# Branch A's attention in slots of one tile, each with a half block of projection

## The chip, the cores and the metric

One core of a Trainium2 chip runs the whole kernel. The time is that of the device for one launch, in microseconds (us), as the median of several runs. The engines named below: TensorE (PE, matmuls; PEld is its weight load), VectorE (DVE), ScalarE (ACT), GpSimd (POOL) and SyncE (SP, whose queue issues the DMAs).

## The reference

A layer with three attention branches over 1024 tokens (two groups of 512) of width 1024. What matters here is branch A, differential attention with 4 heads (the kernel's units), each with two softmax maps over 64 columns, and the gating of each branch:

```python
h = rms_norm(x, pre_g)
u = h @ w_in        # aq ak av ag | bq bk bv bg | cq ck cv cg | mg
logits = einsum('bqhmd,bkhmd->bhmqk', qb, k) * scale + bias      # branch A
p = softmax(logits, axis=-1)
attn = p[:, :, 0] - lam * p[:, :, 1]
o = einsum('bhqk,bkhe->bqhe', attn, v)
ya = rms_norm(o, subln_g) * (1.0 - lambda_init) * silu(ag)
m = gates[0] * (ya @ wa) + gates[1] * (yb @ wb) + gates[2] * (yc @ wc)
x = x + rms_norm(m @ w_out, post_g)
```

Then branches B (grouped queries with rotary embedding) and C (neighbourhood attention), an output projection and an embedding follow.

## The kernel before

Every float32 operand of a matmul is split into a high part and a low part, and a product is three passes: high by high, high by low, low by high. A weight block (128 x 1024) comes by DMA into one of two `stage` slots (`load_w`, L304), ScalarE casts it into `w_hi` (`split_w`, L996 to L1002), GpSimd subtracts to get `w_lo` (`split_w`, L445 to L450). The blocks are numbered: 16 of branch A (query, key, value, gate of 4 units), then key, query 0 and value of branch B, then the blocks of the three merges (a gate projection and a branch projection for each of 8 chunks). A program is written for each engine, and its instructions run in the order written; semaphores with counts join the engines.

`project` (L586) makes one block: 8 chunks k, each with 3 parts by 2 groups of 512 tokens, 48 passes, into two banks of PSUM. A unit of branch A in `attend_qkv` (L667) and `finish` (L699) has eight query tiles of 128. For each tile:

- `score` (L602): six matmuls into two banks, which of two pairs by the tile's parity
- VectorE `find_max` (L1368): bias added and maximum taken (L1383) twice, then the small negation of the two maxima (L1388)
- ScalarE `exp_probs` (L1007, L1017), VectorE `scales` (reciprocal, L1394, and the product with lambda, L1397), ScalarE `scale_second` (L1038), VectorE `norm_probs` (L1411)
- TensorE `turn_probs` (L615, L618): four transposes
- ScalarE `probs_hi` (L1029) and VectorE `probs_lo` (the subtraction of L1355)

With the tiles come the passes of the unit's own gate block in the shares of `GATE_SHARES_A` (one or two of 8 chunks in a tile). The blocks of query, key and value of the next unit stand behind the tiles, in `finish` and behind it, with `mix_group` (L663), which mixes the values of a group by the turned tiles, between them, and `sum_squares` (L713) last. The three units in a loop and the last one are written at L791 to L801. In the last unit the blocks are those of branch B.

Behind the units (L802 to L838): GpSimd takes the power of all 32 columns of the squares' sums (`inv_sqrt`, L433, L482), then of the 16 of the keys' heads, then splits the next gate blocks. VectorE makes eight diagonals (L1634), TensorE spreads them by a product with ones (L819) between the chunks of a block, and VectorE normalises y (L1641). Two gate blocks of merge A and three turns follow, the keys' rotated turn (L827) ahead of the second gate block (L831). ScalarE and VectorE split keys, values and y (`split_y`) while that block runs. Then `merge_branch` and `merge_rest` (L743) alternate branch products and gate blocks; the first gate block of `merge_rest` is the third of the merge.

## Time and profile before

| | |
|---|---|
| median of 3 runs | 1528.74 us (1524.14 to 1530.47) |
| span of the profiled execution | 1522.4 us |
| PE busy | 1411.3 us, 93% |
| DVE busy | 602.4 us, 40% |
| ACT busy | 536.9 us, 35% |
| POOL busy | 291.8 us, 19% |
| TensorE in the chain that ended last | 84% of the span |

The busy time is of one profiled execution; matmuls are pipelined, so that a matmul of about 0.39 us is followed by the next after 0.23 us, and distances between starts tell what a pass costs. "Idle before, releaser" in a row is the time for which the engine stood before the instruction, and whom it waited for. The granted clock is a share of 2.4 GHz: at 0.5 TensorE runs at 1.2 GHz.

### The profile page before, as it was taken

How to read it: one execution, taken by the hardware profiler on the slowest of the kernel's cores; microseconds unless marked ns; L12 is line 12 of the kernel's file. 1: busy time of each engine (PE TensorE's matmuls, PEld its weight loads, DVE VectorE, ACT ScalarE, POOL GpSimd, SP SyncE). 2: the span in 40 equal slices, each digit the busy share in tenths (PEclk: the TensorE clock that was granted, in tenths of full speed). 3: DMA queues.
4: the chain of work that ended last, by engine and by line, in shares of the span. 5: the costliest groups of instructions: out<-in, count | busy, mean ns of one | idle time of the engine just before them, and what ended most of it. 6: DMA issues, size and time to landing. Idle time of an engine off the chain costs nothing.

```text
span 1522.4 us, 18598 instructions
## 1 busy us (share of the span) xinstructions
PE 1411.3 (93%) x6780; PEld 1129.2 (74%) x6780; DVE 602.4 (40%) x1062; ACT 536.9 (35%) x977; POOL 291.8 (19%) x173
## 2 busy tenths in 40 slices
PE   5999999999999798987999898989898999899998
PEld 3767677677887576765788786878787888788887
DVE  5272635546300646456212125152525212544332
ACT  4262534432111536446211115252524212324432
POOL 1211202131222113020022131111211112213100
PEclk9999999999999999998999999999999999999999
DMA  5111101011111000000011110111000113322200
GB/s 185 57 36 36 49 21 49 28 45 46 42 42 55 28 14 28 14 14 8 21 43 61 55 56 23 46 34 34 34 28 29 42 42 138 111 82 70 69 35 35
DMA packets 25746, 71.77 MB, mean 47 GB/s; under 512 B 2872, under 2 KB 4792, under 8 KB 25568
## 3 DMA queue, kind: packets, MB, share of 16 engines
q1 hardware_dynamic: 25696, 71.09, 13.9%
q8 instruction: 33, 0.54, 0.2%
q14 instruction: 17, 0.14, 0.0%
HBM read 66.86 MB, written 4.23 MB: 47 GB/s over the span
## 4 chain that ended last, share of the span: by engine, by line
PE 84%; DVE 8%; ACT 3%; issue 3%; POOL 1%; DMA 0%; SPq 0%; DVEq 0%; ACTq 0%; POOLq 0%
PE ps L581 45%; PE ps L738 9%; PE ps L633 7%; PE ps L952 6%; PE ps L934 6%; PE ps L618 3%; PE ps L611 3%; ACT s L1017 2%; DVE s L1383 2%; PE ps L598 2%; PE ps L958 1%; DVE pt_lo L1355 1%; DVE stat L1388 1%; PE ps L764 1%; POOL small L436 1%
## 5 line engine op out<-in xcount | busy, mean ns | idle before, releaser
L450 POOL TENSOR_TENSOR w_lo<-stage,w_hi 128x1024 fp32r<-128x1024 f32 (+1 forms) x92 | 194.4, 2113 | 923.8 <-ACT w_hi L1002 922.6
L581 PE MATMUL ps<-h_hi,w_hi 128*128 128x512 f32 x1040 | 335.8, 404 | 4.2 <-ACT s L1017 1.9
L581 PE MATMUL ps<-h_lo,w_hi 128*128 128x512 f32 x1040 | 324.3, 393 | 0.0
L581 PE MATMUL ps<-h_hi,w_lo 128*128 128x512 f32 x1040 | 323.7, 393 | 0.0
L581 PEld LDWEIGHTS ps<-h_hi,w_hi 128*128 128x128 f32 x1040 | 188.6, 189 | 59.2 <-issue 19.7
L581 PEld LDWEIGHTS ps<-h_lo,w_hi 128*128 128x128 f32 x1040 | 196.5, 189 | 44.5
L581 PEld LDWEIGHTS ps<-h_hi,w_lo 128*128 128x128 f32 x1040 | 196.3, 189 | 43.3
L1002 ACT CAST w_hi<-stage 128x1024 fp32r<-128x1024 f32 (+1 forms) x92 | 86.0, 935 | 298.2 <-PE ps L581 213.1
L1029 ACT CAST pt_hi<-ps 128x512 fp32r<-128x512 f32 (+2 forms) x160 | 77.6, 525 | 167.6 <-PE ps L618 103.6
L1355 DVE TENSOR_TENSOR pt_lo<-ps,pt_hi 128x512 fp32r<-128x512 f32 (+2 forms) x160 | 91.3, 603 | 113.9 <-ACT pt_hi L1029 113.9
L618 PE MATMUL ps<-ident,s 128*128 128x128 f32 x544 | 85.6, 288 | 51.5 <-DVE pt_lo L1355 34.4
L618 PEld LDWEIGHTS ps<-ident,s 128*128 128x128 f32 x544 | 63.9, 146 | 80.7 <-DVE pt_lo L1355 32.1
L1383 DVE CUSTOM_DVE_ANT_0 s<-ps,tables 128x512 f32<-128x512 f32 (+2 forms) x128 | 70.5, 588 | 91.3 <-PE ps L611 64.0
L1017 ACT ACTIVATE s<-s,stat 128x512 f32<-128x512 f32 (+2 forms) x128 | 81.2, 636 | 55.0 <-DVE stat L1388 54.6
L1502 DVE SCALAR_TENSOR_TENSOR s<-s,ps 128x1024 f32<-128x1024 f32 x16 | 19.5, 1221 | 190.1 <-PE ps L738 190.1
L633 PE MATMUL ps<-pt_hi,v_hi 128*128 128x512 f32 (+2 forms) x192 | 71.0, 370 | 9.1 <-DVE pt_lo L1355 4.8
L738 PE MATMUL ps<-pt_hi,w_hi 128*128 128x512 f32 x192 | 61.7, 404 | 10.3 <-DVE m L1504 8.9
L633 PE MATMUL ps<-pt_lo,v_hi 128*128 128x512 f32 (+2 forms) x192 | 69.1, 360 | 0.0
L633 PE MATMUL ps<-pt_hi,v_lo 128*128 128x512 f32 (+2 forms) x192 | 68.6, 357 | 0.0
L1038 ACT ACTIVATE s<-s,stat 128x512 f32<-128x512 f32 (+2 forms) x96 | 65.0, 677 | 4.4 <-DVE stat L1394 4.4
L738 PE MATMUL ps<-pt_hi,w_lo 128*128 128x512 f32 x192 | 60.9, 399 | 0.0
L738 PE MATMUL ps<-pt_lo,w_hi 128*128 128x512 f32 x192 | 60.7, 398 | 0.0
(173 smaller groups left out, 1881.6 us busy)
## 6 DMA issues: line engine op xcount, KB each, us to landing
stage<-in_w_gates SPq DMA_DIRECT2D x24, 512.0 KB, 3.2
stage<-in_w_qkvg_a SPq DMA_DIRECT2D x19, 512.0 KB, 3.2
stage<-in_w_qkvg_c SPq DMA_DIRECT2D x16, 512.0 KB, 3.2
stage<-in_w_branch SPq DMA_DIRECT2D x24, 256.0 KB, 2.7
m<-in_x_tok SPq DMA_DIRECT2D x4, 1024.0 KB, 9.4
y<-in_x_tok SPq DMA_DIRECT2D x8, 512.0 KB, 3.4
stage<-in_w_pg SPq DMA_DIRECT2D x16, 256.0 KB, 2.7
out<-y SPq DMA_DIRECT2D x16, 256.0 KB, 2.0
```

Of the source, the lines that this page charges most:

```text
L450: nc.gpsimd.tensor_tensor(dst, stage[:, slot, 0:width], f32(hi), ALU.subtract).then_inc(w_ready, 1)
L581: done = mm(ps[:, bank + g, :], w[:, slot, k * P:(k + 1) * P], h[:, k, g * SEQ:(g + 1) * SEQ], start=first and part == 0, stop=last and pa ...
L618: done = nc.tensor.transpose(ps[:, e if both else t % 2, k * P:(k + 1) * P], s[:, t % 2, e, k * P:(k + 1) * P], ident[:, :])
L633: done = mm(ps[:, 2 + g, q0 * P:q1 * P], v[:, g * QT + k, e * HD:e * HD + P], p[:, e if both else g, k, q0 * P:q1 * P], start=n == 0, stop ...
L738: done = mm(ps[:, 2 + g, :], w[:, slot, c * P:(c + 1) * P], yy[:, c * TOK + g * SEQ:c * TOK + (g + 1) * SEQ], start=c == 0 and part == 0, ...
L934: done = mm(ps[:, 2 * c + nb, :], a[:, k * P:(k + 1) * P], w[:, k, nb * 512:(nb + 1) * 512], start=k == 0 and part == 0, stop=k == KC - 1 ...
L952: mm(ps[:, c, :], a[:, k * P:(k + 1) * P], w[:, k * 512:(k + 1) * 512], start=k == 0 and part == 0, stop=k == KC - 1 and part == 2)
L1002: nc.scalar.copy(dst, stage[:, slot, 0:width]).then_inc(w_hi_done, 1)
L1017: done = nc.scalar.activation(dst, src, ACT.Exp, bias=stat[:, t % 2, 2 + e:3 + e], accum_out=stat[:, t % 2, 4 + e:5 + e])
L1029: nc.scalar.copy(*turned_probs(pt_hi, j, near, both, e)) \
L1355: sub = lambda out, whole, hi: nc.vector.tensor_tensor(out, whole, f32(hi), ALU.subtract)
L1383: done = nc.vector.tensor_tensor_reduce(out=s[:, t % 2, e, 0:width], in0=ps[:, 4 + 2 * (t % 2) + e, 0:width], in1=bias[:, e, first:first + ...
```

## The change

Branch A is cut into 32 tile slots without a loop. A slot has the next tile's score, 24 passes (one group's half of a block of the next half unit: query, key, value, gate in slots 0 to 3 of a half), and the turn of the slot's own tile. A block's weights are thus used by one group at a time and are loaded, cast and split twice, once for each group (32 blocks of A where there were 16). Scores use one pair of banks, projections banks 6 and 7 in turn, and the mix of a half stands at the end of its fourth slot. Sums, powers, diagonals and the normalisation of y are made per half or per unit, inside the slots of the next unit; the last two of the eight are left for the tail. The bias is kept in two places by turns, the second in `m`. The last four slots carry branch B's key block and the first gate block of merge A. In the tail stand the value block, the query block, and the second gate block, now ahead of the three turns. `LATER` in place of `LEAD` is a count's offset only.

TensorE:

```diff
+            def project_a(slot, chunks):
+                half, j = block_of(slot)
+                n, g, bank = N_A + 4 * half + j, half % 2, 6 + j % 2
+                if 0 in chunks:
+                    pe.wait_ge(w_ready, LEAD + n + 1)
...
+                    if j == 0:
+                        pe.wait_ge(v_ready, LEAD + half)
+                    if j == 1:
+                        pe.wait_ge(gate_ready, LEAD + half)
...
+                for k in chunks:
+                    for part, (w, h) in enumerate([(w_hi, h_hi), (w_hi, h_lo), (w_lo, h_hi)]):
+                        done = mm(ps[:, bank, :], w[:, n % 2, k * P:(k + 1) * P], h[:, k, g * SEQ:(g + 1) * SEQ],
+                                  start=k == 0 and part == 0, stop=k == KC - 1 and part == 2)
...
+            def turn_values_a(half):
+                g = half % 2
+                pe.wait_ge(plain, LEAD + half + 1)
...
+            def score_a(tile):
...
+                if tile >= 1:
+                    pe.wait_ge(maxed, LEAD + tile)
...
+            def turn_tile_a(tile):
+                pe.wait_ge(normed, LEAD + tile + 1)
+                if tile >= 2:
+                    pe.wait_ge(pt_ready, LEAD + tile - 1)
...
+            def mix_a(half):
...
+                pe.wait_ge(v_ready, LEAD + half + 1)
+                pe.wait_ge(pt_ready, LEAD + 4 * half + 4)
+                mix(g, False, False)
...
+            def spread_rstd(c, bank):
+                pe.wait_ge(diag_ready, LEAD + c + 1)
+                if c == 0:
+                    pe.wait_ge(ones_ready, LEAD + 1)
+                pe.wait_ge(y_normed, LEAD + c)
...
+            def attend_a(tile):
+                half, j = divmod(tile, 4)
+                u, t = divmod(tile, 8)
+                fill = project_a if tile < A_TILES - 4 else project_next
+                if tile + 1 < A_TILES:
+                    score_a(tile + 1)
+                if j < 3:
+                    fill(tile, range(0, KC // 2))
+                    if j == 1 and half >= 1:
+                        sum_squares(half - 1)
+                    if u >= 1 and t in (4, 5):
+                        spread_rstd(2 * (u - 1) + t - 4, 3)
+                    fill(tile, range(KC // 2, KC))
+                    turn_tile_a(tile)
+                else:
+                    fill(tile, range(0, 2))
+                    if half + 1 < A_HALVES:
+                        turn_values_a(half + 1)
+                    fill(tile, range(2, 5))
+                    turn_tile_a(tile)
+                    fill(tile, range(5, KC))
+                    mix_a(half)
...
+            project_a(-3, range(KC))
+            project_a(-2, range(KC))
+            score_a(0)
+            project_a(-1, range(0, 4))
+            turn_values_a(0)
+            project_a(-1, range(4, KC))
+            for tile in range(A_TILES):
+                attend_a(tile)
+            pe.wait_ge(w_ready, LEAD + N_KQV + 3)
+            pe.wait_ge(maxed, LEAD + A_TILES)
+            for k in range(KC):
+                done = project_part(0, 4, k, k == 0, k == KC - 1)
+                if k == 3:
+                    pe.wait_ge(pt_ready, LEAD + A_TILES)
+                    turn(rope_buf, 0, turned)
+                if k == 5:
+                    sum_squares(A_HALVES - 1)
...
+            pe.wait_ge(w_ready, LEAD + N_KQV + 4)
+            pe.wait_ge(mg_tanh, LEAD + 1)
             for k in range(KC):
                 done = project_part(1, 6, k, k == 0, k == KC - 1)
+                if k == 4:
+                    pe.wait_ge(ss_saved, LEAD + A_HALVES)
+                    spread_rstd(A_HALVES - 2, 2)
+                if k == 6:
+                    spread_rstd(A_HALVES - 1, 3)
...
-            project(N_MERGE[0], 1, 4)
+            pe.wait_ge(plain, LATER + UNITS + 2)
+            project(N_MERGE[0] + 1, 0, 4)
             pe.wait_ge(roped, LEAD + 1)
             turn(rope_buf, 0, rope_turned)
-            pe.wait_ge(y_normed, LEAD + 8)
+            pe.wait_ge(y_normed, LEAD + A_HALVES)
             turn(vg, 2, turned)
-            pe.wait_ge(plain, LEAD + UNITS + 3)
-            project(N_MERGE[0] + 1, 0, 6)
-            pe.wait_ge(k_ready, LEAD + UNITS + 1)
+            pe.wait_ge(plain, LATER + UNITS + 3)
+            pe.wait_ge(k_ready, LATER + UNITS + 1)
             turn(rope_buf, 0, turned)
```

GpSimd:

```diff
+            for n in range(4 * A_HALVES):
+                split_w(N_A + n, n % 2)
+                u, slot = divmod(n, 8)
...
+                if u + 1 < UNITS and slot in (6, 7):
+                    spread_bias_a(u + 1, slot - 6)
+                if u >= 1 and slot == 7:
+                    square_root_a(u - 1)
+            split_w(N_KQV, 0)
+            split_w(N_KQV + 1, 1)
+            split_w(N_KQV + 2, 0)
             pool.wait_ge(mixed, LEAD + 2 * UNITS)
...
+            square_root_a(UNITS - 1)
...
             pool.wait_ge(head_var, LEAD + 1)
             inv_sqrt(head_rstd, head_ss, head_pow)
-            for f in range(2):
-                split_w(N_MERGE[0] + f, 1 - f)
+            split_w(N_KQV + 3, 1)
+            split_w(N_MERGE[0] + 1, 0)
```

ScalarE:

```diff
+            def attend_a(tile):
+                half, j = divmod(tile, 4)
+                if j != 0:
+                    probs_hi_a(tile - 1)
+                if tile <= A_TILES - 4:
+                    take_block_a(*block_of(tile - 1))
+                else:
+                    take_next(tile - 1)
+                if tile < A_TILES - 4:
+                    split_w(N_A + tile + 5, (tile + 1) % 2, (tile + 5) // 2 + 1)
+                if tile == A_TILES - 4:
+                    split_w(N_KQV + 1, 1, N_KQV // 2 + 1)
+                if tile == A_TILES - 2:
+                    split_w(N_KQV + 2, 0, N_KQV // 2 + 2)
+                if j == 0 and half >= 1:
+                    square_output(half - 1)
+                if tile + 1 < A_TILES:
+                    exp_a(tile + 1)
+                    scale_second_a(tile + 1)
+                if j == 3:
+                    if half + 1 < A_HALVES:
+                        values_hi_a(half + 1)
+                    probs_hi_a(tile)
```

VectorE:

```diff
+            def attend_a(tile):
+                half, j = divmod(tile, 4)
+                u, t = divmod(tile, 8)
+                if tile + 1 < A_TILES:
+                    find_max_a(tile + 1)
+                if j != 0:
+                    probs_lo_a(tile - 1)
+                if tile <= A_TILES - 4:
+                    take_block_a(*block_of(tile - 1))
+                if tile + 1 < A_TILES:
+                    scales_a(tile + 1)
+                    norm_probs_a(tile + 1)
+                if j == 0 and half >= 1:
+                    take_y_a(half - 1)
+                if j == 2 and half >= 1:
+                    save_squares(half - 1)
+                if u >= 1 and t in (3, 4):
+                    diagonal(2 * (u - 1) + t - 3)
+                if u >= 1 and t in (5, 6):
+                    normalize_y(2 * (u - 1) + t - 5, 3)
+                if j == 3:
+                    if half + 1 < A_HALVES:
+                        values_lo_a(half + 1)
+                    probs_lo_a(tile)
```

SyncE loads the weights of A in the order of the 32 half blocks, each waiting for the split of the block two before, with the bias rows between them:

```diff
+            for n in range(2, 4 * A_HALVES):
+                load_w(N_A + n, n % 2, w_qkvg_a[4 * (n // 8) + n % 4])
+                u, slot = divmod(n, 8)
+                if n == 3:
+                    load_raw_a(0, 1)
+                if u + 1 < UNITS and slot in (5, 7):
+                    load_raw_a(u + 1, slot // 6)
```

## Rows read from the trace of the kernel before

**Rows 1.** Windows (start:end us, length, busy PE PEld DVE ACT POOL, clock, DMA); a PE gap.

```profile
69.00:334.46 265.46, 249.85 (x1216) 192.14 (x1213) 133.26 (x313) 122.50 (x234) 43.82 (x23) 0.97 0.11 38
...
870.00:874.00 4.00, 3.52 (x9) 2.80 (x10) 0.43 (x1) 0.00 (x0) 0.00 (x0) 0.57 0.38 131
...
870.48 1.22 PE L738 MATMUL ps<-pt_hi,w_hi 128*128 128x512 f32 x2 [4.69 <-DVE m L1504]
```

**Rows 2.** Waits of TensorE, 40 to 560 us (us in total, times, longest).

```profile
PE ps L618 <- DVE s L1411: 9.0, 8, 1.8
```

**Rows 3.** Chain of work that ended last (start us, us, what).

```profile
168.37 5.51 PE ps L581 x24
...
180.27 2.74 PE ps L633 x12
...
207.70 1.68 PE ps L720 x16
...
340.40 0.89 DVE m L1634 x4
...
393.19 10.99 PE ps L581 x48
```

**Rows 4.** Timeline of PE in unit 1 (start us, us, instruction): turn, score, projection.

```profile
152.57 0.60 PE L618 MATMUL ps<-ident,s 128*128 128x128 f32 x4
153.10 0.50 PE L611 MATMUL ps<-k_hi,q_hi 64*128 64x512 f32 x2
...
153.99 0.74 PE L581 MATMUL ps<-h_hi,w_hi 128*128 128x512 f32 x2
```

**Rows 5.** Timelines of ScalarE and GpSimd: the second weight block's cast and subtraction.

```profile
39.38 1.05 ACT L1002 CAST w_hi<-stage 128x1024 fp32r<-128x1024 f32 x1
...
40.51 2.38 POOL L450 TENSOR_TENSOR w_lo<-stage,w_hi 128x1024 fp32r<-128x1024 f32 x1 [11.52 <-ACT w_hi L1002]
```

**Rows 6.** Timelines of PE and DVE: unit 1's first score, maximum, negation.

```profile
139.90 0.50 PE L611 MATMUL ps<-k_hi,q_hi 64*128 64x512 f32 x2
...
141.16 0.69 DVE L1383 CUSTOM_DVE_ANT_0 s<-ps,tables 128x512 f32<-128x512 f32 x1 [0.88 <-PE ps L611]
...
142.50 0.17 DVE L1388 TENSOR_SCALAR stat<-stat 128x2 f32<-128x2 f32 x1
```

**Rows 7.** Timelines of PE and ACT: a turn and its copy.

```profile
148.24 0.65 PE L618 MATMUL ps<-ident,s 128*128 128x128 f32 x4 [1.74 <-DVE v_lo L1355]
...
148.93 0.59 ACT L1029 CAST pt_hi<-ps 128x512 fp32r<-128x512 f32 x1 [1.05 <-PE ps L618]
```

**Rows 8.** Timelines of POOL and DVE; last, line 1411's durations (ns min/median/max).

```profile
157.44 2.38 POOL L450 TENSOR_TENSOR w_lo<-stage,w_hi 128x1024 fp32r<-128x1024 f32 x1 [28.36 <-ACT w_hi L1002]
...
158.28 1.57 DVE L1388 TENSOR_SCALAR stat<-stat 128x2 f32<-128x2 f32 x1
...
161.43 0.17 DVE L1394 RECIPROCAL stat<-stat 128x2 f32<-128x2 f32 x1 [0.34 <-ACT s L1017]
...
L1411 DVE SCALAR_TENSOR_TENSOR s<-s,stat x32: 737/746/2382, 74.9 to 314.7; 128x512 f32<-128x512 f32 x32
```

**Rows 9.** Timelines of four engines behind the units, up to the merge.

```profile
334.95 8.28 POOL L436 TENSOR_TENSOR small<-small 128x32 f32<-128x32 f32 x2 [8.00 <-DVE small L1366]
...
372.48 1.04 PE L598 MATMUL ps<-ident,tables 128*128 128x128 f32 x8
...
376.79 1.05 ACT L1138 ACTIVATE s<-ps 128x1024 f32<-128x1024 f32 x1
...
378.81 4.63 DVE L1355 TENSOR_TENSOR pt_lo<-y,pt_hi 128x1024 fp32r<-128x1024 f32 x4 [1.15 <-ACT pt_hi L1132]
...
387.77 1.03 ACT L1066 ACTIVATE y<-ps 128x1024 f32<-128x1024 f32 x1 [6.16 <-PE ps L598]
...
389.81 2.41 POOL L450 TENSOR_TENSOR w_lo<-stage,w_hi 128x1024 fp32r<-128x1024 f32 x1 [11.52 <-ACT w_hi L1002]
```

**Rows 10.** The page's DMA issues (KB each, us to landing).

```profile
stage<-in_w_qkvg_a SPq DMA_DIRECT2D x19, 512.0 KB, 3.2
```

More of the change, by code:

```diff
@@ new lines, in sum_squares @@
+            def sum_squares(half):
+                g = half % 2
+                pe.wait_ge(y_ready, LEAD + half + 1)
+                for qt in range(QT):
+                    done = mm(ps[:, 2 + g, 2 * qt:2 * qt + 2], y_squares[g][:, qt * P:(qt + 1) * P], ones2,
+                              start=True, stop=True)
+                done.then_inc(ss_done, 1)
+            def spread_rstd(c, bank):
[3 more added lines that the diff above has]
+                pe.wait_ge(y_normed, LEAD + c)
+                for qt in range(QT):
+                    done = mm(ps[:, bank, qt * P:(qt + 1) * P], ones_sq, diagonals[c % 2][:, qt * P:(qt + 1) * P],
+                              start=True, stop=True)
+                done.then_inc(spread, 1)
@@ L812, in _ @@
-            pe.wait_ge(ones_ready, LEAD + 1)
-            squares_taken(UNITS)
-            pe.wait_ge(w_ready, LEAD + N_KQV + 3)
-            for c in range(2 * UNITS):
-                pe.wait_ge(diag_ready, LEAD + c + 1)
-                pe.wait_ge(y_normed, LEAD + c - 1)
-                for qt in range(QT):
-                    done = mm(ps[:, 2 + c % 2, qt * P:(qt + 1) * P], ones_sq,
-                              diagonals[c % 4][:, qt * P:(qt + 1) * P], start=True, stop=True)
-                done.then_inc(spread, 1)
-                done = project_part(0, 4, c, c == 0, c == KC - 1)
@@ new lines, in exp_a, with scale_second_a @@
+            def exp_a(tile):
+                act.wait_ge(maxed, LEAD + tile + 1)
+                for e in range(2):
+                    dst = s[:, tile % 2, e, :]
+                    done = nc.scalar.activation(dst, dst, ACT.Exp, bias=stat[:, tile % 2, 2 + e:3 + e],
+                                                accum_out=stat[:, tile % 2, 4 + e:5 + e])
+                done.then_inc(exped, 1)
+            def scale_second_a(tile):
+                act.wait_ge(scales_ready, LEAD + tile + 1)
+                p1 = s[:, tile % 2, 1, :]
+                nc.scalar.mul(p1, p1, stat[:, tile % 2, 8:9]).then_inc(scaled, 1)
@@ new lines, in scales_a, with norm_probs_a @@
+            def scales_a(tile):
+                st = stat[:, tile % 2, :]
+                dve.wait_ge(exped, LEAD + tile + 1)
+                steps.done(dve, nc.vector.reciprocal(st[:, 6:8], st[:, 4:6]))
+                nc.vector.tensor_tensor(st[:, 8:9], st[:, 7:8], lam, ALU.mult).then_inc(scales_ready, 1)
+            def norm_probs_a(tile):
+                st = stat[:, tile % 2, :]
+                p0, p1 = s[:, tile % 2, 0, :], s[:, tile % 2, 1, :]
+                dve.wait_ge(scaled, LEAD + tile + 1)
+                stt(out=p0, in0=p0, scalar=st[:, 6:7], in1=p1, op0=ALU.mult, op1=ALU.subtract).then_inc(normed, 1)
@@ new lines, in save_squares, with diagonal @@
+            def save_squares(half):
+                dve.wait_ge(ss_done, LEAD + half + 1)
+                nc.vector.tensor_copy(a_ss[:, 4 * half:4 * half + 4], ps[:, 2 + half % 2, 0:8:2]).then_inc(ss_saved, 1)
+                if half % 2 == 1:
+                    dve.wait_ge(ss_saved, LEAD + half + 1)
+                    mean_square(a_ss[:, 4 * half - 4:4 * half + 4], P, a_var)
+            def diagonal(c):
+                dve.wait_ge(y_pow, LEAD + c // 2 + 1)
+                if c == 0:
+                    dve.wait_ge(x_turned, LEAD + TILES)
+                if c >= 2:
+                    dve.wait_ge(spread, LEAD + c - 1)
+                for qt in range(QT):
+                    done = nc.vector.tensor_scalar(diagonals[c % 2][:, qt * P:(qt + 1) * P], ident[:, :],
+                                                   a_rstd[:, 4 * c + qt:4 * c + qt + 1], None, ALU.mult)
+                done.then_inc(diag_ready, 1)
```

487 lines of the change are left out of this document (287 added, 200 removed).

## The prediction, made before the changed kernel was run

> **What bounds the kernel now.** I read the windows by stage first. From 69.00 to 334.46, the four units of branch A, TensorE is busy 249.85 of 265.46 us at a granted clock of 0.97 [rows 1]. So at most 15.6 us of idle time is to be had there, and some 3.4 us of clock (about four of the 4 us windows at 0.57 to 0.80, where matmuls run at 1.2 instead of 2.4 GHz). The waits of TensorE say who ends the idle time: the turn of a tile waits for the normalised tile, 9.0 us in 8 waits [rows 2]. VectorE and ScalarE run a serial chain per tile that the eight tile slots of a unit hardly cover, while the long stretches after them leave both idle. The change spreads the projections evenly over the slots. Everything up to 393.19, where the third gate projection of merge A begins in the kernel before [rows 3], is touched; behind it the code is the same. I work out when that projection starts in the changed kernel.
>
> **TensorE's work is conserved.** A turn takes 0.53 us to the next score (153.10 - 152.57), a score 0.89 us to the projection behind it (153.99 - 153.10), 24 passes 5.51 us, and restarting them costs about 0.1 us (estimate, from the first pair's length) [rows 3, 4]. A slot is then 0.53 + 0.89 + 5.51 + 0.1 = 7.03 us. The passes work on one group instead of two, so each pair of passes no longer shares a weight; but the mix, where each pass has its own weights, runs at 2.74 / 12 = 0.228 us a pass, the projection at 5.51 / 24 = 0.230 [rows 3]. Nothing is added there. The loop: 32 slots 225.0; less the last score 1.0; seven half turns of values at 0.5, 3.5; eight mixes at 2.8, 22.4; seven sums of squares at 1.68 / 2 and a restart, 6.3; six spreads at 1.0 (half the passes of a sum, 0.84, and restarts), 6.0 [rows 3]. Sum 262.2 us.
>
> **The ramp.** The first half block is done at about 39.8 as before. K's block needs the weights whose low part GpSimd finishes at 40.51 + 2.38 = 42.9 [rows 5]; before, TensorE had the second group of the first block to do meanwhile. K and V, 5.6 each, end at 54.1; score 0, 0.9; half of the gate block, 2.8, to 57.8. The turn of the values waits for a copy that stands behind tile 0's exponentials on ScalarE: their maximum comes at about 56.7, collides with a weight split (below) until 57.7, 1.5 for the exponentials, 0.5 for the copy, so 59.8, a 2.0 us wait. Then 0.5 + 2.8: slot 0 starts at 63.0. Loop without waits: to 63.0 + 262.2 = 325.2.
>
> **The chain in a slot, and what it meets.** Count from the start of a slot's score (S). The maximum starts at S + 1.26 (141.16 - 139.90), the small negation behind it at S + 2.60 (142.50) [rows 6]. Meanwhile ScalarE: the turn before is 0.53 old at S and its copy starts 0.69 after it (148.93 - 148.24), S + 0.16; some 0.5 later (the copy lasts 0.59) that of the projected block, as much later the weight cast, and GpSimd's subtraction starts 1.13 after a cast (40.51 - 39.38), S + 2.25 [rows 5, 7]. It runs 2.4 us. The trace shows what a negation does then: it started at 158.28 inside the subtraction of 157.44 to 159.82 and took 1.57 instead of 0.17 us, to 159.85; over the trace the normalisation's length, too, goes from 737 to 2382 ns [rows 8]. Before, that happens once a unit; now each slot but the last few has a weight subtraction at that place, 0.35 us ahead of the negation. The negation ends at S + 4.7, the reciprocal follows 1.58 later (161.43 - 159.85) [rows 8], the scaling of the second map ends at S + 7.5, the normalisation at S + 8.2. Without the collision it is S + 6.2. Either fits, since the tile is wanted a slot later.
> The Trainium skill, page SBUF — State Buffer, section Who interferes with whom, says that an operation of VectorE in a 2-port mode such as tensor_scalar, and GpSimd, take a shared port pair as an exclusive lock, whoever issues first. The trace agrees, the negation above. By that page it is the order of issue that decides; were there no such lock, the first rival's time would hold.
>
> **Two places where TensorE waits for the end of that chain.**
> First, the fourth slot of each half: VectorE splits the values and the fourth turned tile behind the next tile's normalisation, and the mix stands on it. 8.2 + 0.7 + 0.7 = S + 9.6 against TensorE's arrival: score 0.9, 24 passes 5.6, turns 0.5 and 0.5, S + 7.5. That is 2.2 us with the wake-up, seven times (the last half has no next tile): 15.4. In three of them a diagonal (0.89 us [rows 3]) stands ahead too, but GpSimd's power shifts its subtraction there; between 0 and 2.6, I take 1.3.
> Second, slot 5 of units 1 to 3: both spreads of the past unit use bank 3, so the second waits for the first to be normalised, which VectorE does behind slot 5's own normalisation. TensorE comes there at S + 0.9 + 2.9 + 0.9 = 4.7; the normalisation of y ends at S + 8.2 + 0.7 = 8.9 with the collision, 6.9 without. Two slots at 4.3 and one, in the last unit where no weights are cast, at 2.2: 10.8. After a gap of 4.69 us the clock was 0.57 for 4 us [rows 1]: the level of 1.2 GHz for most of them. Such a gap costs about 1.5 us more, twice: 3.0. A copy of K's block adds 0.4. The loop ends at 325.2 + 15.4 + 1.3 + 10.8 + 3.0 + 0.4 = 356.1.
>
> **What follows the loop.** V's block with a turn (0.9), the last sum (0.9) and restarts: 13.0. The query's weights stand in GpSimd's queue behind two powers. The sum starts at 9.2 after the loop, is saved and scaled by 10.8; powers of 32 and 16 columns take 8.28 together [rows 9], so 8 and 16 take 1.5 and 2.8, with the squares' reduction (1.2) between them hidden by half; subtraction 2.4 (2.41 in [rows 9]). Ready at 17.7: a wait of 4.7, and 1.5 of clock. Query block with two spreads 13.0, gate block 11.0: the turn of the rotated keys starts 43.2 after the loop. Before, a gate block of 11 us stood behind that turn and covered ScalarE and VectorE; now it stands ahead. Before, the first y_lo came 378.81 - 372.48 = 6.33 after the turn, 0.92 of it a tanh that is gone, and four took 4.63 [rows 9]: the last at 10.05. Then ScalarE squares and casts, and the third gate's weights are ready 389.81 + 2.41 - 387.77 = 4.45 later [rows 9]: 14.6, with wake-ups 15.0. The gate starts at 356.1 + 43.2 + 15.0 = 414.3, 21.1 later than 393.19.
> Branch A's weights once more are 16 loads of 512 KB and 3.2 us to landing each [rows 10], one per slot of 7 us and asked for two slots ahead: hidden. SyncE's bias rows stand between them; raw rows take about 5 us and have two slots. The 16 more casts (0.94) and subtractions (2.4) lie beside TensorE, and cost what the collision costs. The bias of two units in two places lets the spreading run early: nothing on the path.
>
> **Sum.** 1522.4 + 21.1 = 1543.5 span; the median of the runs is 6.3 above the profiled span (1528.74 - 1522.4): 1549.8, **1550 us**.
>
> **Rivals.** *No collision* (0.19): the negation slips in ahead of the subtraction, which decides from 0.35 us of shift in my reading [rows 6, 7]. Mix waits 0.2 x 7, slot 5's 2.2 x 3, clock none: the loop ends at 63.0 + 262.2 + 1.4 + 6.6 + 0.4 = 333.6, the gate starts at 391.8, and the time is 1527: not slower. For it: the difference of two paths each read to 0.1 us. Against: ScalarE starts each slot early.
> *The pipeline is full* (0.12): I have a wait wrong, TensorE never waits in the loop: 325.2 + 58.2 = 383.4, -9.8, 1519; if the tail's waits (4.7 + 1.5) go too, 1513. For it: the sum of engine time per slot is far under 7 us on ScalarE and VectorE. Against: the order of each queue, above.
> *More of it* (0.14): clock lost at each mix gap too (7 x 1.5 = 10.5), the diagonals in full (1.3), GpSimd's copies of the bias in the way (3 x 1): 1565.
> The change does what it says in all of them; that it doesn't is no case, the slots are written out.
>
> **How the numbers follow.** My case 0.55, around 1550 (1542 to 1557 by itself). A measurement tells about 0.5% from no change, 7.6 us: 1521.1 to 1536.4. Slower: 0.55 + 0.14 = 0.69. Same: no collision, less the 0.02 in which it ends below, 0.17, and a sixth of the full pipeline, 0.02: 0.19. Faster 0.12. For 8 in 10 the range goes from the no-collision case less 6 us, 1521, to 1563.
>
> **What would show it.** In the profile after: waits of TensorE at the mix for VectorE's pt_lo, seven near 2.2 us; in slot 5 of units 1 to 3 a wait of the spread for VectorE's y, 4.3 us; a wait of about 5 us for a weight subtraction behind V's block; the negation lengthened to near 2.2 us in most slots. First score near 54, slot 0 at 63, the loop's end near 356. If the negation is 0.17 us in most slots, my case is wrong and the first rival right; if TensorE's idle time between 63 and the merge is under 10 us, the second is.

## The result and the profile after

The changed kernel takes **1551.29 us** (median of 4 runs, 1551.13 to 1551.55) against 1529.01 for the kernel before on the same chip (4 runs, 1524.14 to 1530.47): a ratio of 1.0161, 95% interval 1.0140 to 1.0182. It is slower by 1.6%; 1550 was predicted. The profiled execution has a span of 1549.2 us where before had 1522.4, so 26.8 us more. The times of the kernel before fall in two groups (in the comparisons of the experiments 26 runs at 1522.7 to 1526.3 with a granted clock of 0.970 to 0.975, and 16 at 1528.4 to 1532.0 with 0.966 to 0.969), so its median moves by a few us from one comparison to the next, and the profiled execution belongs to the first group.

The page of the changed kernel: busy time of each engine; the chain that ended last, by engine; the traffic to and from HBM; the weight loads of branch A (KB each, us to landing).

```profile
PE 1420.4 (92%) x6780; PEld 1135.2 (73%) x6780; DVE 629.0 (41%) x1085; ACT 556.0 (36%) x1015; POOL 328.0 (21%) x192
...
PE 80%; DVE 10%; ACT 5%; issue 3%; POOL 1%; DMA 0%; SPq 0%; DVEq 0%; ACTq 0%; POOLq 0%
...
HBM read 75.25 MB, written 4.23 MB: 51 GB/s over the span
...
stage<-in_w_qkvg_a SPq DMA_DIRECT2D x35, 512.0 KB, 3.3
```

The share of TensorE in the chain fell from 84 to 80%. The doubled loads are 35 instead of 19 [rows 10] and land as fast as before, 3.3 us; none of the waits of TensorE from 40 to 440 us has a DMA for its releaser. The waits of TensorE from 40 to 440 us (us in total, times, longest) answer to [rows 2]:

```profile
PE ps L667 <- DVE pt_lo L1579: 12.7, 7, 2.1
PE ps L846 <- DVE y L1795: 10.7, 3, 4.2
PE ps L615 <- POOL w_lo L468: 5.2, 2, 4.5
PE ps L763 <- POOL w_lo L468: 3.1, 1, 3.1
...
PE ps L791 <- ACT vg L1237: 1.9, 1, 1.9
...
PE ps L781 <- ACT tables L1251: 0.4, 1, 0.4
```

The 9.0 us for turns in [rows 2] are gone. In their place the mix (L667) stands seven times for the low parts, the spread (L846) three times for y, and there are waits for GpSimd's weights at the ramp (L763) and behind the loop (L615). The 1.9 us (L791) are the first turn of the values, and the 0.4 us (L781) are for ScalarE's copy of branch B's key block. A slot with the 4.2 us wait, and the negation over the whole trace, from the timelines of GpSimd, VectorE and TensorE (start us, us, instruction, idle time before and releaser); the last line gives ns min/median/max:

```profile
177.36 2.40 POOL L468 TENSOR_TENSOR w_lo<-stage,w_hi 128x1024 fp32r<-128x1024 f32 x1 [10.65 <-ACT w_hi L1132]
...
177.69 2.10 DVE L1718 TENSOR_SCALAR stat<-stat 128x2 f32<-128x2 f32 x1
...
184.08 2.05 PE L846 MATMUL ps<-m 128*128 128x128 f32 x8 [4.20 <-DVE y L1795]
...
L1718 DVE TENSOR_SCALAR stat<-stat x32: 168/2094/2312, 58.1 to 344.9; 128x2 f32<-128x2 f32 x32
```

The negation of two columns starts 0.33 us inside GpSimd's subtraction and ends with it, 2.10 us long. That was one tile in eight before; now the median of all 32 is 2.09 us. Chain of the work that ended last, changed kernel (start us, us, what), from the ramp to branch B; it answers to [rows 3]:

```profile
42.83 12.87 PE ps L763 x48
55.70 0.92 PE ps L808 x6
...
64.85 0.90 PE ps L808 x5
...
358.55 5.50 PE ps L615 x24
...
375.80 9.92 PE ps L615 x30
...
417.36 11.24 PE ps L615 x48
...
523.67 0.89 PE ps L632 x8
...
527.95 5.94 PE ps L615 x18
```

Line 55.70 is score 0, 64.85 slot 0's score, 358.55 the end of the loop of slots, and 417.36 the third gate block of merge A, which stood at 393.19 [rows 3]: 24.2 us later. Merge A itself ends 24.4 later (523.67 against 499.23), the first unit of branch B adds some 2.3, and from there the distance stays (merge C's start 892.85 against 865.90: 26.95).

### The profile page after: what moved, and what is told of

It reads as the page before. It is cut to its first block, busy times and chain, and to the rows that moved or that the text cites. A ratio compares the mean times of both kernels' runs of the same rounds, so it can differ in the third digit from the quotient of the medians.

```text
span 1549.2 us, 18441 instructions
## 1 busy us (share of the span) xinstructions
PE 1420.4 (92%) x6780; PEld 1135.2 (73%) x6780; DVE 629.0 (41%) x1085; ACT 556.0 (36%) x1015; POOL 328.0 (21%) x192
## 4 chain that ended last, share of the span: by engine, by line
PE 80%; DVE 10%; ACT 5%; issue 3%; POOL 1%; DMA 0%; SPq 0%; DVEq 0%; ACTq 0%; POOLq 0%
PE ps L615 34%; PE ps L888 8%; PE ps L667 8%; PE ps L763 7%; PE ps L1081 6%; PE ps L1063 6%; PE ps L652 3%; PE ps L645 2%; DVE pt_lo L1579 2%; DVE stat L1718 2%; ACT s L1269 2%; PE ps L808 2%; PE ps L632 2%; PE ps L1087 1%; PE ps L781 1%
## 5 line engine op out<-in xcount | busy, mean ns | idle before, releaser
L468 POOL TENSOR_TENSOR w_lo<-stage,w_hi 128x1024 fp32r<-128x1024 f32 (+1 forms) x108 | 232.3, 2152 | 911.0 <-ACT w_hi L1132 910.8
L615 PE MATMUL ps<-h_hi,w_hi 128*128 128x512 f32 x768 | 246.3, 402 | 7.2 <-POOL w_lo L468 5.2
L615 PE MATMUL ps<-h_lo,w_hi 128*128 128x512 f32 x768 | 239.9, 394 | 0.0
L615 PE MATMUL ps<-h_hi,w_lo 128*128 128x512 f32 x768 | 239.6, 393 | 0.0
L1132 ACT CAST w_hi<-stage 128x1024 fp32r<-128x1024 f32 (+1 forms) x108 | 103.0, 955 | 307.3 <-PE ps L615 211.2
L615 PEld LDWEIGHTS ps<-h_hi,w_hi 128*128 128x128 f32 x768 | 140.7, 189 | 43.8 <-issue 9.9
L615 PEld LDWEIGHTS ps<-h_lo,w_hi 128*128 128x128 f32 x768 | 145.2, 189 | 32.7
L615 PEld LDWEIGHTS ps<-h_hi,w_lo 128*128 128x128 f32 x768 | 145.4, 189 | 32.2
L763 PE MATMUL ps<-h_hi,w_hi 128*128 128x512 f32 x256 | 107.5, 420 | 6.4 <-POOL w_lo L468 6.4
L1159 ACT CAST pt_hi<-ps 128x512 fp32r<-128x512 f32 (+2 forms) x128 | 59.1, 511 | 134.7 <-PE ps L652 69.7
L763 PE MATMUL ps<-h_hi,w_lo 128*128 128x512 f32 x256 | 102.5, 400 | 0.0
L763 PE MATMUL ps<-h_lo,w_hi 128*128 128x512 f32 x256 | 101.8, 398 | 0.0
L667 PE MATMUL ps<-pt_hi,v_hi 128*128 128x512 f32 (+2 forms) x192 | 71.7, 373 | 21.8 <-DVE pt_lo L1579 17.6
L888 PE MATMUL ps<-pt_hi,w_hi 128*128 128x512 f32 x192 | 62.4, 408 | 12.7 <-DVE m L1844 8.9
L1269 ACT ACTIVATE s<-s,stat 128x512 f32<-128x512 f32 x64 | 45.7, 716 | 71.7 <-DVE stat L1718 71.7
L667 PE MATMUL ps<-pt_lo,v_hi 128*128 128x512 f32 (+2 forms) x192 | 69.7, 363 | 0.0
L667 PE MATMUL ps<-pt_hi,v_lo 128*128 128x512 f32 (+2 forms) x192 | 69.2, 360 | 0.0
L763 PEld LDWEIGHTS ps<-h_hi,w_hi 128*128 128x128 f32 x256 | 49.3, 193 | 26.4 <-issue 10.7
```

What stands on the lines that cost most here:

```text
L468: nc.gpsimd.tensor_tensor(dst, stage[:, slot, 0:width], f32(hi), ALU.subtract).then_inc(w_ready, 1)
L615: done = mm(ps[:, bank + g, :], w[:, slot, k * P:(k + 1) * P], h[:, k, g * SEQ:(g + 1) * SEQ], start=first and part == 0, stop=last and pa ...
L667: done = mm(ps[:, 2 + g, q0 * P:q1 * P], v[:, g * QT + k, e * HD:e * HD + P], p[:, e if both else g, k, q0 * P:q1 * P], start=n == 0, stop ...
L763: done = mm(ps[:, bank, :], w[:, n % 2, k * P:(k + 1) * P], h[:, k, g * SEQ:(g + 1) * SEQ], start=k == 0 and part == 0, stop=k == KC - 1 a ...
L888: done = mm(ps[:, 2 + g, :], w[:, slot, c * P:(c + 1) * P], yy[:, c * TOK + g * SEQ:c * TOK + (g + 1) * SEQ], start=c == 0 and part == 0, ...
L1132: nc.scalar.copy(dst, stage[:, slot, 0:width]).then_inc(w_hi_done, 1)
```

## The experiments

The times are medians; each ratio is to the kernel before on the same chip in the same comparison (1525.78 us of 20 runs for the first four, 1524.77 of 13 for the next four, 1524.97 of 9 for the last two). The ratio of the changed kernel is 1.0161. "Loop excess" is the distance from slot 0's score to the loop's end, less the 262.2 us that the prediction summed for TensorE's own work in it.

**1. The negation in a form that the subtraction does not block** (changed kernel).

```diff
-nc.vector.tensor_scalar(st[:, 2:4], st[:, 0:2], -1.0, None, ALU.mult).then_inc(maxed, 1)
+nc.vector.tensor_reduce(st[:, 2:4], st[:, 0:2].unsqueeze(2), AX.X, ALU.max,
+                        negate=True).then_inc(maxed, 1)
```

> The changed kernel, with the negation behind each maximum of branch A (line 1718, a tensor_scalar that lasts 2.1 to 2.3 us in most slots) written as a tensor_reduce with negate; nothing else. My theory (the collision with GpSimd's weight subtraction sets the end of the chain): the negation lasts under 0.3 us in every slot, TensorE's wait at the mix falls from 12.7 us in 7 to under 3, its wait for y in slot 5 from 4.2 to about 2.2 us in the first two units, and the time falls by 12.7 - 2 + 4 + 3 (clock) = 17 to 19 us, to 1533. Rival (the collision fills slack that the chain has anyway, and the chain is simply too long for a slot): no more than 3 us are gained, 1548 or more. Rival (the doubled loads, casts and subtractions cost by themselves): no change, 1551.

Measured: 1531.54 us (1530.75 to 1533.18), ratio 1.0034 (1.0019 to 1.0049); span 1529.9, 19.3 less than the changed kernel's. Negation (ns), then TensorE's waits from 40 to 440 us:

```profile
L1718 DVE TENSOR_REDUCE stat<-stat x32: 154/155/156, 58.7 to 326.3; 128x2 f32<-128x2 f32 x32
...
PE ps L846 <- DVE y L1796: 6.8, 3, 2.3
...
PE ps L667 <- DVE pt_lo L1579: 2.2, 3, 0.7
```

The subtractions are all still there, 2.4 us each, and at the same place: in the slot shown above the reduction starts at 183.32 in a subtraction of 183.00 to 185.42, and takes 0.15. The mix waits drop from 12.7 to 2.2 and those for y from 10.7 to 6.8, 2.3 at the longest (predicted for this case: 0.2 and 2.2 each). Without the collision 19.8 of the some 25 us of loss are gone.

**2. y normalised at the head of its slot** (changed kernel): on VectorE the normalisation of y stands ahead of the next tile's maximum, no longer behind the tile's normalisation. The collision stays.

```diff
+if u >= 1 and t in (5, 6):
+    normalize_y(2 * (u - 1) + t - 5, 3)
 if tile + 1 < A_TILES:
     find_max_a(tile + 1)
 ...
-if u >= 1 and t in (5, 6):
-    normalize_y(2 * (u - 1) + t - 5, 3)
```

> The changed kernel, with VectorE's normalisation of y in slots 5 and 6 of units 1 to 3 moved from behind that slot's chain to the head of the slot; nothing else. My theory (two spreads share bank 3, and the second waits for a step queued behind slot 5's chain): the three waits of the spread for y (10.7 us in all, 4.2 at the longest) vanish, and the half-rate clock behind two or three of them with it (1.5 us each): 13.5 to 15 us less, 1537. Rival (the wait is only given on to the mix of the next slots, where the same chain is late): the mix's waits grow by what is gained and the time stays at 1549 or more.

Measured: 1534.43 us (1532.78 to 1538.63), ratio 1.0061 (1.0038 to 1.0085); span 1533.0. The wait of L846 is gone; the mix keeps its own:

```profile
PE ps L667 <- DVE pt_lo L1579: 12.8, 7, 2.1
```

The loop goes from 63.51 to 344.25, an excess of 18.5 us where the changed kernel has 31.5: 10.7 for the waits, and 2.3 net for the clock. Net, because the clock now falls behind three of the mix waits (0.76 from 128 to 132 us, 0.72 from 200, 0.68 from 272), where in the changed kernel it fell behind one. Of the 16.2 us of span another 1.3 came ahead of the loop and 1.9 behind it, where no edit lies: K's block took 11.27 instead of 12.87 us, and the 30 matmuls behind the wait for the query's weights 8.74 instead of 9.92. So the time, 2.6 us under the 1537 of the theory, holds about 3 us that the edit doesn't explain.

**3. Both.**

> Both edits together (negation as tensor_reduce, y normalised at the head of slots 5 and 6). My theory: TensorE's waits in the loop fall to under 5 us, the loop ends near 331, and the time is 1551 - 18 - 10 = 1522 to 1526 (the wait in slot 5 is counted once: what is left of it after the first edit is 3 x 2.2 and some clock). Rival (either edit uncovers a third wait of the same size): no better than the better of the two alone, 1532 or more.

Measured: 1519.68 us (1518.74 to 1521.73), ratio 0.9958 (0.9945 to 0.9972); span 1516.5. TensorE's wait at the mix (the only other one inside the loop is the 0.4 for the copy of the key block), and, from the chain, slot 0's score and the loop's end:

```profile
PE ps L667 <- DVE pt_lo L1579: 2.2, 3, 0.7
...
62.95 0.89 PE ps L808 x6
...
328.09 5.50 PE ps L615 x24
```

The loop takes 265.1 us, an excess of 2.9, of which 2.6 are these two waits. So 262.2 was right for TensorE's own work to 0.3 us, and the pipeline of slots does what it is for once the two places are cleared. It beats the kernel before, by 0.4%. The two edits bring 31.6 us together, where they bring 19.8 and 16.9 one by one: the long waits for y were made of both, the collision and the place in the queue. The 1522 to 1526 that were expected were too slow.

**4. A shorter subtraction.** Changed kernel; from the third block of branch A on, GpSimd subtracts 512 of 1024 columns, so that half of the low parts of those weights isn't made. The negation keeps its form.

```diff
-split_w(N_A + n, n % 2)
+split_w(N_A + n, n % 2, width=TOK if n < 2 else 512)
```

> The changed kernel, with GpSimd's subtraction for branch A's weights over 512 of 1024 columns from the third block on: the other half of the low parts isn't computed (old values are used). Loads, casts, matmuls and every wait stay. A dose of the suspected cause: a subtraction of 1.3 instead of 2.4 us still starts 0.3 us ahead of the negation. My theory: the negation lasts 1.0 to 1.2 instead of 2.1 to 2.3 us, the mix's seven waits fall by 1.1 each (7.5 us), slot 5's by 1.1 twice (2), with some of the clock: 10 us less, 1541. Rival (GpSimd's work doesn't matter): no change, 1551.

Measured: 1542.42 us (1540.25 to 1544.71), ratio 1.0115 (1.0087 to 1.0143); span 1538.0.

```profile
L1718 DVE TENSOR_SCALAR stat<-stat x32: 168/993/2101, 57.6 to 334.6; 128x2 f32<-128x2 f32 x32
...
PE ps L667 <- DVE pt_lo L1579: 8.9, 7, 2.7
PE ps L846 <- DVE y L1795: 8.5, 3, 3.1
```

The subtraction lasts 1.29 to 1.30 us and the median negation 0.99; the waits for y fall from 4.2 to 3.1 at the longest, by what the negation is shorter. The length of the wait follows the length of the subtraction, with the instruction on VectorE unchanged. The longest mix wait rose to 2.7, though. It is the last one (it ends at 309.98), and its negation is blocked for 2.09 us as before: it starts at 302.27, in a subtraction of 301.94 to 304.33 that belongs to branch B's key block and isn't shortened. In the changed kernel the same negation fell into the power ahead of that subtraction and took 0.17 us.

**5. The query's weights ahead of the powers on GpSimd** (changed kernel).

```diff
+split_w(N_KQV + 3, 1)
 square_root_a(UNITS - 1)
 ...
-split_w(N_KQV + 3, 1)
 split_w(N_MERGE[0] + 1, 0)
```

> The changed kernel, but on GpSimd the subtraction of the last query-weight block of branch A is issued ahead of the two powers of the last unit instead of behind them. In the changed kernel's trace the powers take 368.95 to 373.44, the subtraction 373.44 to 375.75, and TensorE waits 4.5 us for it; the clock is 0.50 in 376 to 380. Theory (the wait is queueing on GpSimd and nothing else): the wait of 4.5 goes, and with it the clock lost behind it (about 1.5), so the marker of merge A comes 5.5 to 6 us earlier and the time is 1545 to 1546; the powers, now 2.3 later, must not become a wait of the last turn. Rival 1 (ScalarE's cast of that block is just as late): the wait shrinks to 1 to 2 and the time is 1548 to 1549. Rival 2 (the branch's end is set by GpSimd's later subtractions, for the gate blocks, whatever stands before): the time stays at 1551.

Measured: 1540.47 us (1539.99 to 1543.04), ratio 1.0096 (1.0063 to 1.0130); span 1538.6, 10.6 less, where 6 was expected.

```profile
367.86 9.74 PE ps L615 x42
...
409.25 11.24 PE ps L615 x48
...
519.85 4.33 PE ps L615 x18
```

Between the sum of squares and the first spread lie 9.7 us here and 17.2 in the changed kernel (368.48 to 385.72): 7.5, of which 4.5 is the wait and 3.0 the clock. In the changed kernel the 30 matmuls behind the wait took 9.92 us, at 0.23 each they are 6.9: I had priced the clock at 1.5. The price isn't the same in every execution: behind the same wait of 4.5 us the 30 matmuls took 9.96 us in experiment 6, 9.47 to 9.59 in 1, 4 and 10, and 8.74 in 2 and 3. The marker comes 8.1 earlier. Of the rest, 1.6 us is in branch B's first unit: the same 18 matmuls take 4.33 instead of 5.94 us.

**6. The second gate block in halves around the turns** (changed kernel).

```diff
-project(N_MERGE[0] + 1, 0, 4)
+project(N_MERGE[0] + 1, 0, 4, range(0, KC // 2))
 pe.wait_ge(roped, LEAD + 1)
 turn(rope_buf, 0, rope_turned)
 pe.wait_ge(y_normed, LEAD + A_HALVES)
 turn(vg, 2, turned)
+project(N_MERGE[0] + 1, 0, 4, range(KC // 2, KC))
```

> The changed kernel, but the second gate block of merge A is issued in two halves: four chunks of rows ahead of the turns of the keys, four behind them, so that the chain of ScalarE and VectorE behind those turns lies beside TensorE's work. The changed kernel's trace has the marker (third gate block) at 417.36 and 15 us between the turn of the keys at 402.48 and it. Theory: the gap is the chain y_lo, cast, subtraction of the gate weights (407.89 + 4.87, 1.05, 2.40), some 4 to 6 us of it without TensorE work at full clock; with the halves it is covered and the time is 1545 to 1546. Rival (the chain is long in any order since GpSimd and VectorE carry it end to end, and the halves only move the idle time): the time is 1549 to 1551.

Measured: 1547.43 us (1546.48 to 1551.32), ratio 1.0143 (1.0107 to 1.0179); span 1545.4, 3.8 less: between theory and rival. The waits between the turn of the keys and the marker fall from 4.7 (1.59, 2.44 and 0.70) to 2.7 (0.25, 0.39 and 2.08). The next thing is late: the chain now runs through SyncE's queue (the weight load from 399.11 to 402.47), which experiment 9 takes up.

**7. The reduction in the kernel before.** The diff of experiment 1, on the kernel before.

> The kernel before, with its negation of the two maxima (128x2) written as a reduction with the sign turned, as in the run of the changed kernel that took the 2.1 us negations away. The trace of before has the blocked negation once a unit (1.55 to 1.65 us against 0.17), four in all. Theory (the collision costs what the chain behind it loses, slot by slot): about 1.4 us for each of the four, 5 to 6 us, with the clock in one or two units perhaps 1 more: 4 to 7 us faster than before, ratio 0.9954 to 0.9974. Rival (slack of the old order takes it up, since each score there stood beside a whole projection): under 1.5 us, ratio over 0.999. If the changed kernel's advantage of the reduction (19.8 us) came from anything but the collisions, this run would also gain far more than 6 us.

Measured: 1523.76 us (1522.13 to 1525.45), ratio 0.9978 (0.9962 to 0.9994). The ratio says some 3 us faster, less than the theory's 4 to 7, but the medians are only 1.0 us apart: all ten runs lie in the lower range of before's times, and the ratio rests on the 5 of 13 runs of before that took over 1528 us. The negations are all at 0.15, yet the waits of the turns fell only from 9.0 to 7.6 us, 1.4 us, which fits the medians. Between the theory and the rival (under 1.5 us) this leaves the rival as the better reading. VectorE and GpSimd in its last unit, and the wait of TensorE:

```profile
298.21 2.38 POOL L450 TENSOR_TENSOR w_lo<-stage,w_hi 128x1024 fp32r<-128x1024 f32 x1 [28.00 <-ACT w_hi L1002]
...
298.97 0.15 DVE L1388 TENSOR_REDUCE stat<-stat 128x2 f32<-128x2 f32 x1
299.28 1.86 DVE L1412 SCALAR_TENSOR_TENSOR s<-s,stat 128x512 f32<-128x512 f32 x1 [0.15 <-ACT s L1038]
...
301.19 0.66 PE L618 MATMUL ps<-ident,s 128*128 128x128 f32 x4 [1.70 <-DVE s L1412]
```

The negation gets through, and the next instruction of VectorE that the subtraction can block, the normalisation (0.74 us elsewhere), stands until the subtraction is over. The turn waits 1.70 instead of 1.84. It is so in all four units (1.86 to 1.87 us each). In experiment 1 it doesn't happen: in the slot at 183 us the normalisation starts 2.9 us behind the negation (186.23, the subtraction ends at 185.42), and all 32 stay at 750 to 754 ns.

**8. Everything that the trace pointed to.** The edits of 1, 2, 5 and 6, and one at the ramp:

```diff
 # ScalarE, in the loop over the x tiles
+if t == 6:
+    split_w(N_A + 1, 1, 1)
 ...
-split_w(N_A + 1, 1, 1)
 split_w(N_A + 2, 0, 2)
```

> The changed kernel with all edits together: the reduction for the negation, y normalised at the head of its slots, the query weights ahead of the powers on GpSimd, the second gate block in halves around the turns, and ScalarE's cast of the second weight block moved ahead of the last x tiles (the trace of the changed kernel has TensorE wait 3.1 us for that block at 39.7 to 42.8, and the clock at 0.58 in 44 to 48). Theory (the waits lie one after the other and add up): 1519.7 for the first two edits as measured, less 6 for the query weights, 5 to 6 for the halves, 3 to 4.5 for the ramp: 1504 to 1506, faster than before by 1.2 to 1.5%. Rival (each wait removed exposes the next engine, so that less than half of the three later gains arrives): 1512 to 1517.

Measured: **1503.78 us** (1502.89 to 1504.25), ratio 0.9853 (0.9821 to 0.9884); span 1500.5. That is 0.2 us under the 1504 to 1506 of the theory. The three later edits bring 15.9 us on top of experiment 3, where they bring 10.8, 3.9 and 5.5 one by one on the changed kernel: most of it arrives, but not the whole sum of 20.2. What TensorE still waits for between 40 and 440 us is under 8 us in all; the longest rows (three more are 0.8, 0.4 and 0.3):

```profile
PE ps L667 <- DVE pt_lo L1581: 2.2, 3, 0.7
PE ps L615 <- POOL w_lo L468: 2.1, 1, 2.1
PE ps L888 <- DVE pt_lo L1581: 1.2, 1, 1.2
...
```

**9. The weight load ahead of the rotation tables on SyncE**, on top of 8.

```diff
+load_w(N_MERGE[0] + 2, 1, w_branch[0])
 sp.wait_ge(roped, LEAD + 1)
 load_rope(q_g, q_g_swapped)
-load_merge_rest(0)
+load_w(N_MERGE[0] + 3, 0, w_gates[2])
+load_merge_rest(0, 1)    # its loop starts at 1
```

> The changed kernel with the five edits, and one more: SyncE issues the load of the first branch weights of merge A ahead of the four loads of the rotation tables, which wait for the rotation of the keys, instead of behind them. In the kernel with the five edits the chain that ends last runs through this queue: VectorE's rotation to 354.37, the table loads 354.39 to 356.1, the weight load issued at 356.55 and landed at 360.75, and ScalarE stands 2.4 us for it ahead of its cast and the casts of y. Theory (after the halves of the gate block, the next thing late is this load): the 2.4 us go, the marker of merge A comes 2 to 2.4 earlier and the time is 1501.4 to 1502.2. Rival 1 (VectorE, not ScalarE, then sets the chain: its split of the values ends only 0.6 to 1 us before): 1 to 1.5 us, 1502.5. Rival 2 (the tables, now 0.5 later, delay the rotation of the query): 1503.8 or more.

Measured: 1502.87 us (1501.99 to 1504.86), ratio 0.9851 (0.9832 to 0.9871). In time that can't be told from experiment 8. The chains show a local gain that the end doesn't keep. First experiment 8, then 9:

```profile
49.91 0.91 PE ps L808 x4
...
356.55 4.20 DMA stage<-in_w_branch
...
371.81 11.23 PE ps L615 x48
...
482.38 4.33 PE ps L615 x18
```

```profile
51.11 0.93 PE ps L810 x4
...
370.52 11.24 PE ps L617 x48
...
481.10 5.94 PE ps L617 x18
```

From score 0 to the marker it is 321.9 us with the load behind the tables and 319.4 with it ahead: 2.5 less, and the DMA is out of the chain. But score 0 came 1.2 later in this execution, where no edit lies, and branch B's first 18 matmuls ran at the lower clock, 5.94 us against 4.33. So the load did stand in the chain, but the total missed the theory (1501.4 to 1502.2) and lies nearest to the first rival's 1502.5; with runs from 1501.99 to 1504.86 it decides nothing.

**10. The ramp alone** (changed kernel with the two lines of experiment 8).

> The changed kernel, but ScalarE casts the second weight block ahead of the last x tiles' work instead of behind it, so that GpSimd's low part is ready when TensorE has done the first half block. In the changed kernel TensorE waits 3.1 us for it (to 42.83) and the clock is 0.58 in 44 to 48. Theory (both are the price of this wait): score 0 comes 4.5 to 5.8 us earlier and the time is 1545.5 to 1547. Rival 1 (the clock falls there whatever the gap): 3 us, 1548.3. Rival 2 (the later slots take the gain back, since the weights' casts or the collision set their pace): score 0 earlier, but the loop's end within 1 us of before, 1550 to 1551.

Measured: 1545.74 us (1545.07 to 1546.53), ratio 1.0131 (1.0108 to 1.0154); span 1543.3. As the theory said:

```profile
51.13 0.91 PE ps L808 x6
...
353.59 5.50 PE ps L615 x24
```

Score 0 is 4.6 us earlier, the loop's end 5.0. The slots take nothing of it back, and both 3.1 us of wait and 1.5 of clock were its price in the changed kernel's execution.

## Why the prediction was right, step by step

**The forecast held**: slower, with the time 1.3 us off, by the mechanism that was named. The signs that it asked for are there: the median negation 2.09 us, mix waits of up to 2.1, waits for y of 4.2 in slot 5, a wait of 4.5 for the query's weights. But that it is only 1.3 us off is luck: the span was 5.7 us too short and the step from span to time 4.2 us too long, and the clock was underpriced at every place. It was so from the first paragraph on: 3.4 us of clock were read in branch A of the kernel before, where a mean clock of 0.97 over 265.46 us [rows 1] says about 8, and the six windows of 4 us below 0.97 (two each of 0.57 and 0.80, one of 0.77 and one of 0.78) add up to 6.8.

- *The collision.* Subtraction 0.35 us ahead of the negation was predicted, 0.33 measured, and experiments 1 and 4 show cause and dose. The chain was read rightly, too: in the slot shown, whose score starts at 175.23, the negation ends at S + 4.6 and the normalisation at S + 8.0 (predicted 4.7 and 8.2). The Trainium skill (SBUF — State Buffer, section Who interferes with whom) says that tensor_reduce never contends with GpSimd on this chip while tensor_scalar in a 2-port mode can; experiment 1 agrees, 155 ns against 2094. The same section of the Trainium skill has VectorE's instructions with two inputs in SBUF contend with a GpSimd instruction that reads SBUF; experiment 7 agrees, 1.86 us against 0.74.
- *TensorE's work conserved.* A slot was to be 7.03 us and is 7.04 (scores at 189.85 and 196.89); the sum 262.2 is confirmed to 0.3 by experiment 3.
- *The ramp.* K's block at 42.9 was right (42.83), score 0 was to come at 54.1 and came at 55.70, slot 0 at 63.0 and at 64.85. The step that failed: the wait of 3.1 us ahead of K's block got no clock term. 1.5 us of it, as experiment 10 shows. In experiments 2 and 3 the same wait cost no clock (K's block in 11.27 and 11.26 us, where 11.2 was predicted).
- *The loop.* Its excess was predicted as 30.9 (356.1 - 63.0 - 262.2) and measured as 31.5 (358.55 - 64.85 - 262.2), but made up otherwise, so that it is only 0.6 off is luck as well. The mix waits are 12.7, not 15.4 and 1.3 for the diagonals: the three with a diagonal ahead are only 1.5 to 1.6 us each, since there the negation fell into the power and wasn't blocked. The y waits are 10.7, as predicted (10.8). With the 0.4 for the copy of the key block the waits are 23.8, so 7.7 are left for the clock, where I had 3.0. The windows of the changed kernel (start:end, length, busy PE PEld DVE ACT POOL, clock, DMA, GB/s) show it low behind the y waits of all three units (in the last one 0.68 from 336 to 340 us), and also at 208, behind a mix wait of 1.96 us that ended at 206.44. The third rival had that, my case had not:

```profile
184.00:188.00 4.00, 3.92 (x15) 3.53 (x16) 0.00 (x0) 0.00 (x0) 0.00 (x0) 0.59 0.00 0
...
208.00:212.00 4.00, 4.00 (x14) 2.53 (x13) 0.00 (x0) 0.60 (x1) 1.15 (x1) 0.60 0.39 131
...
260.00:264.00 4.00, 2.07 (x9) 2.10 (x10) 1.41 (x2) 0.34 (x1) 0.00 (x0) 0.50 0.09 38
```

- *The tail.* The wait for the query's weights was put at 4.7 and was 4.5; the clock behind it at 1.5 and was 3.0 in this execution (experiment 5). The terms that I gave for the weights add up to 18.1 us behind the loop, not to 17.7; they were ready at 17.2 (375.75 - 358.55). From the loop's end to the turn of the keys 43.2 was predicted and 43.9 measured (402.48 - 358.55), then 15.0 and 14.9 to the marker. It stands at 417.36, predicted 414.3: 3.1 late, 1.9 of it at the ramp, 0.6 in the loop, 0.6 in the tail.
- *"Behind it the code is the same."* The code is, the clock isn't. The unit of branch B that follows merge A ran its first 18 matmuls in 5.94 us where before had 4.35, and with the rest of the unit some 2.3 us came on top. This term was missing, and experiment 5 has the 18 back at 4.33 us without any edit there.
- *From span to time.* I added 6.3 us, the median of the runs less the span of one execution. In the kernels run since, a profiled execution's own time is 1.8 to 2.4 above its span (1525.45 and 1523.7 in experiment 7, 1551.13 and 1549.2 in the changed kernel), so the page's execution of before can only have been the one of 1524.14: 1.7 lies around the span, and the other 4.6 is the distance between the two groups of the kernel before. So the span was underestimated by 5.7 (1543.5 against 1549.2), and a 4.2 us error in this term made up for most of it.

**The rivals.** *No collision* was priced at 1527; with the collision taken away it is 1531.5. The size of the rival was off, not its mechanism: of the 18.6 us that the loop's end came earlier (358.55 to 339.99) I had forecast 22.5 (356.1 to 333.6). The y waits that stay, 6.8 us, still cost clock: the loop excess is 13.4 for 9.4 us of waits. *The pipeline is full* was priced at 1519 and is 1519.7 once both places are cleared (experiment 3), so what the slots could bring was read rightly from the trace of before. *More of it* is half true: clock was lost at mix gaps, but not at all seven (at one in the changed kernel, at three in experiment 2).

**What is left open.** Why the clock falls behind one gap and not behind the next is not settled. The 3.1 us gap at the ramp is the same in experiments 1 and 2; K's 48 matmuls behind it took 12.86 us in the first and 11.27 in the second. Branch B's 18 matmuls took 4.33 to 4.35 in the kernel before and in experiments 3, 5 and 8, 5.71 to 5.80 in 1, 2, 4 and 10, and 5.94 in the changed kernel and in 6 and 9. By which rule it falls can't be said from these traces. It bounds what any such sum can promise: the ramp's gap cost nothing in some executions and 1.6 to 1.7 us in others, and the wait for the query's weights between 1.8 and 3.1 (8.74 to 9.96 us for 30 matmuls that take 6.9 at 0.23).

## What to carry to other kernels

When work is spread evenly over slots, every slot gets the same coincidences: a collision that cost one slot in eight before now costs every slot, so put the instructions of VectorE and GpSimd of one slot on one time axis before trusting the sums of busy time. Look at the smallest instructions of the chain first: here 128x2 elements, 0.17 us, decided over 1.2% of the kernel's time, and writing them as a reduction gave that back. When you free one instruction from such a block, check that the next one in line starts outside it (experiment 7), and when a wait goes, look again at every queue for what is late next (experiments 6 and 9).

## What the runs showed of the hardware that I had not expected

A product of 128x1 elements with both inputs in SBUF is blocked as well, and the power on GpSimd did not block the negation. In slot 3 of unit 1 of the changed kernel the negation runs inside the power untouched (and in the kernel before a tensor_scalar of VectorE took 0.18 us at 337.73, inside powers of 334.95 to 343.23). The reciprocal then runs untouched inside the subtraction, and the product with lambda (L1725, 0.16 us elsewhere) stands until that is over:

```profile
156.60 1.63 POOL L454 TENSOR_TENSOR small<-small 128x8 f32<-128x8 f32 x1 [3.00 <-DVE small L1590]
158.20 2.41 POOL L468 TENSOR_TENSOR w_lo<-stage,w_hi 128x1024 fp32r<-128x1024 f32 x1
...
157.89 0.17 DVE L1718 TENSOR_SCALAR stat<-stat 128x2 f32<-128x2 f32 x1
...
159.65 0.17 DVE L1724 RECIPROCAL stat<-stat 128x2 f32<-128x2 f32 x1 [1.00 <-ACT s L1269]
159.85 0.78 DVE L1725 TENSOR_TENSOR stat<-stat,small 128x1 f32<-128x1 f32 x1
```

A subtraction of VectorE with one operand in PSUM ran at its usual 0.68 us inside GpSimd's in experiment 1 (at 183.39, GpSimd from 183.00 to 185.42). And one and the same wait of 4.5 us cost 1.8 us of clock in two runs and 3.0 in the changed kernel: a price for the clock taken from a single earlier gap, as I took 1.5 from [rows 1], can be half of what the next gap costs.
